# Moving the first quarter of the combined activations 64 bytes up in on-chip memory, onto the remainder of the weights that meet it

## The reference

```python
def conv_ffn(h, w_up, conv_w, conv_b, w_down):
    up = depthwise_conv(h @ w_up, conv_w, conv_b, FFN_CONV // 2)
    g, v = jnp.split(up, 2, axis=-1)
    return (jax.nn.gelu(g, approximate=True) * v) @ w_down

hx2 = modulate(rms_norm(x, g_ffn_pre[l]), sh2, sc2)
x = x + gt2 * rms_norm(conv_ffn(hx2, w_up[l], conv_ffn_w[l], conv_ffn_b[l], w_down[l]), g_ffn_post[l])
```

## Time and profile before

| what | value |
|---|---|
| median of three executions | 2101.1 us (2100.09 to 2101.67) |
| the profiled execution | 2102.9 us, span of its instructions 2101.1 us |
| TensorE matmul busy | 2066.7 us, 98% of the span |
| TensorE weight load busy | 1767.6 us, 84% |
| VectorE, ScalarE, GpSimd busy | 1529.7, 812.0, 79.0 us |
| granted TensorE clock, mean | 0.996 of full |

### The profile page before, as it was taken

One profiled execution on the slowest core, in us unless ns is written; L12 is line 12 of the kernel. 1 busy time (PEld: TensorE's weight loads), 2 busy tenths in 40 slices (PEclk: granted clock), 3 DMA queues, 4 the chain that ended last, 5 costly groups with the idle time before them and its releaser, 6 DMA issues.

```text
span 2101.1 us, 28297 instructions
## 1 busy us (share of the span) xinstructions
PE 2066.7 (98%) x11682; PEld 1767.6 (84%) x11682; DVE 1529.7 (73%) x2202; ACT 812.0 (39%) x1077; POOL 79.0 (4%) x145
## 2 busy tenths in 40 slices
PE   7999999999999999999999999999999999999998
PEld 4678887888777888888889898898988888888887
DVE  5567978876979886767767676676776768577577
ACT  5347576543323352423324243242333324233243
POOL 0000000001110000000000000000000000000002
PEclk9999999999999999999999999999999999999999
DMA  9953424434876524333333333434333333233342
GB/s 394 408 205 111 156 93 163 136 110 169 322 269 230 181 90 140 101 121 119 104 131 104 124 112 109 131 101 140 101 120 121 101 126 101 95 101 101 100 179 103
DMA packets 86193, 311.19 MB, mean 148 GB/s; under 512 B 9456, under 2 KB 13552, under 8 KB 84016
## 3 DMA queue, kind: packets, MB, share of 16 engines
q1 hardware_dynamic: 67824, 243.09, 33.3%
q0 software_dynamic: 17424, 65.50, 9.4%
q10 hardware_dynamic: 816, 0.79, 0.1%
HBM read 300.95 MB, written 8.39 MB: 147 GB/s over the span
## 4 chain that ended last, share of the span: by engine, by line
PE 68%; DVE 2%; DMA 1%; issue 1%; ACT 0%; DVEq 0%; ACTq 0%
PE bank L996 23%; PE bank L998 22%; PE bank L997 22%; DMA ada_raw<-in_adabg 1%; DVE w_lo L1540 1%; DVE acc L2175 0%; PE bank L1107 0%; DVE ada_acc L1572 0%; PE bank L1321 0%; DMA w_raw<-in_stream 0%; DVE x L1880 0%; DVE prod L1891 0%; ACT w_hi L610 0%; DVE ss L1548 0%; PE bank L1292 0%
## 5 line engine op out<-in xcount | busy, mean ns | idle before, releaser
L996 PE MATMUL bank<-h_hi,w_hi 128*128 128x512 f32 (+1 forms) x1968 | 711.1, 361 | 5.9 <-ACT acc L855 2.0
L997 PE MATMUL bank<-h_lo,w_hi 128*128 128x512 f32 (+1 forms) x1968 | 708.1, 360 | 0.0
L998 PE MATMUL bank<-h_hi,w_lo 128*128 128x512 f32 (+1 forms) x1968 | 706.5, 359 | 0.0
L1540 DVE TENSOR_TENSOR w_lo<-w_raw,w_hi 128x1024 fp32r<-128x1024 f32 x260 | 316.0, 1222 | 159.4 <-ACT w_hi L610 159.1
L996 PEld LDWEIGHTS bank<-h_hi,w_hi 128*128 128x128 f32 x1968 | 370.4, 188 | 65.5 <-issue 11.0
L610 ACT ACTIVATE w_hi<-w_raw 128x1024 fp32r<-128x1024 f32 x260 | 273.2, 1056 | 388.6 <-DMA w_raw<-in_stream 388.6
L998 PEld LDWEIGHTS bank<-h_hi,w_lo 128*128 128x128 f32 x1968 | 370.2, 188 | 56.8
L997 PEld LDWEIGHTS bank<-h_lo,w_hi 128*128 128x128 f32 x1968 | 372.8, 189 | 49.0
L996 PE MATMUL bank<-act_hi,w_hi 128*128 128x512 f32 (+1 forms) x688 | 265.0, 385 | 1.9 <-DVE acc L2147 1.5
L997 PE MATMUL bank<-act_lo,w_hi 128*128 128x512 f32 (+1 forms) x688 | 264.3, 384 | 0.0
L998 PE MATMUL bank<-act_hi,w_lo 128*128 128x512 f32 (+1 forms) x688 | 264.2, 384 | 0.0
(11 more groups left out here) (340 smaller groups left out, 2707.8 us busy)
## 6 DMA issues: line engine op xcount, KB each, us to landing
w_raw<-in_stream SPq DMA_DIRECT2D x340, 512.0 KB, 3.5
ada_raw<-in_adabg POOLq DMA_DIRECT2D x112, 512.0 KB, 4.7
ada_raw<-in_ada SPq DMA_DIRECT2D x64, 512.0 KB, 13.6
x<-in_x_t SPq DMA_DIRECT2D x4, 1024.0 KB, 8.4
acc<-in_adabg SPq DMA_DIRECT2D x8, 512.0 KB, 6.3
x<-in_x_t POOLq DMA_DIRECT2D x4, 1024.0 KB, 9.0
x_kept_d<-x SPq DMA_DIRECT2D x4, 1024.0 KB, 5.6
c<-in_ctx_t SPq DMA_DIRECT2D x2, 1024.0 KB, 14.1
```

The costliest lines, as they stand in the source:

```text
L996: t.matmul(out, w, v, start=start, stop=False)
L997: t.matmul(out, w, v_l, start=False, stop=False)
L998: return t.matmul(out, w_l, v, start=False, stop=stop)
L1540: v.tensor_tensor(lo_unit(n), raw_unit(n), hi_unit(n).bitcast(F32), ALU.subtract).then_inc(lo_done, 1)
```

## The change

The four quarters of `t` were one array of 4 x 768 elements, all at remainder 0. Now the array is 64 elements wider, the first quarter begins at element 16 (remainder 64 bytes) and the other three begin at 64 + 768 q (remainder 0, as before). The two arrays grow by 256 bytes each (`t_raw` and `t_lo` share one space). `up_sum` and `sums1_raw`/`sums1_lo` move up by 512 bytes, and the gap ahead of `acc` shrinks by that, so that `acc` and all behind it stay. No instruction, wait or transfer is added, removed or moved in order.

```diff
+T_AT = [16] + [64 + 3 * H * _q for _q in range(1, 4)]
+T_WIDTH = 4 * 3 * H + 64
...
-        t_raw, t_lo = twice(fin, "t_raw", "t_lo", [P, 4, 3 * H])
-        t_hi = sbuf(fin, "t_hi", [P, 4, 3 * H], F32R)
+        t_raw, t_lo = twice(fin, "t_raw", "t_lo", [P, T_WIDTH])
+        t_hi = sbuf(fin, "t_hi", [P, T_WIDTH], F32R)
         up_sum = sbuf(fin, "up_sum", [P, 2 * L])
         sbuf(fin, "gap_to_sums", [P, ASIDE])
         sums1_raw, sums1_lo = twice(fin, "sums1_raw", "sums1_lo", [P, NSUM])
-        sbuf(fin, "gap_to_x1", [P, 256 - ASIDE])
+        sbuf(fin, "gap_to_x1", [P, 256 - ASIDE - 128])
...
+        def three_of(t, q):
+
+            return t[:, ds(T_AT[q], 3 * H)]
+
+        def one_of(t, q, i):
+
+            return t[:, ds(T_AT[q] + i * H, H)]
...
-                a.activation(t_hi[:, q, :], t_raw[:, q, :], ACT.Copy).then_inc(t_rounded, 1)
+                a.activation(three_of(t_hi, q), three_of(t_raw, q), ACT.Copy).then_inc(t_rounded, 1)
...
-                    t4 = t_hi[:, q, 2 * H:3 * H], t_lo[:, q, 2 * H:3 * H]
+                    t4 = one_of(t_hi, q, 2), one_of(t_lo, q, 2)
...
-                    t2, t3 = ((t_hi[:, q, i * H:i * H + H], t_lo[:, q, i * H:i * H + H]) for i in range(2))
+                    t2, t3 = ((one_of(t_hi, q, i), one_of(t_lo, q, i)) for i in range(2))
...
-                t2, t3, t4 = (t_raw[:, q, i * H:i * H + H] for i in range(3))
+                t2, t3, t4 = (one_of(t_raw, q, i) for i in range(3))
...
-                v.tensor_tensor(t_lo[:, q, :], t_raw[:, q, :], t_hi[:, q, :].bitcast(F32), ALU.subtract).then_inc(t_ready, 1)
+                v.tensor_tensor(three_of(t_lo, q), three_of(t_raw, q), three_of(t_hi, q).bitcast(F32), ALU.subtract).then_inc(t_ready, 1)
```

## The result

The changed kernel takes 2089.85 us, the median of four executions (2089.1 to 2093.26), against 2101.16 us for the kernel before (2100.09 to 2101.67). The ratio is 0.9946, with a 95% interval of 0.9935 to 0.9958: 11.3 us or 0.5% faster. The forecast was no change that counts, 2101.9 us, and 2100.1 to 2103.8.

What follows compares the result with a forecast made beforehand. The prediction took TensorE's matmuls, busy throughout the feed-forward stage, as the bound. It summed +0.8 (matmuls) + 0 (making t) + 0 (moved sums) onto 2101.1 for 2101.9 us, range 2100.1 to 2103.8.

Steps and rivals of the forecast that it cites:

- What bounds the stage: Feed-forward stage, 750 to 2031 us: matmuls busy for all 1281.00 us, so every nanosecond of pitch goes into the time.
- The counts: Matmuls reading quarter 0: 9 in a pair, 360 in the kernel, one quarter of the 1440 that read `t`.
- The price at a lasting equal remainder: 256-column matmuls at equal remainders take 120.0 ns in the last down product, against 117.7 ns in the seven products.
- The moved sums: `up_sum` and the second set of sums move by 512 bytes and keep their remainders: zero cost.
- the instructions that make `t`: ScalarE's rounding (848 ns) and VectorE's subtracting (952 ns), near 730 us: costed at nothing, under 32 us of cover.
- The reason given for the sums: Matmuls against these sums and against ring slots show the same 281 ns and no idle time, so distance has no price.
- the 281 ns: Mean duration of the stage's matmul groups by shape, called no price because it overlaps with the next matmul.
- Price at steady pitch: Quarter 0's matmuls in the seven products: 360 x 2.3 ns = 0.8 us added, the prediction's own value.
- Rival 3: A small gain: short runs at equal remainders keep the early short pitch, 2100.7 us; chance 0.04.
- Rival 5: Faster by over 0.2%: 360 matmuls would need a pitch of 106 ns; chance 0.03, anything unforeseen included.
- the switching rival (4): Each of four switches of moving-operand remainder in a pair costs 0.033 us: 5.3 us, 2106.4 us; chance 0.05.

Runs made afterwards that it cites:

- e7: Kernel before, with the units of the seven products and their sums at remainder 0, so all 84 matmuls of a pair at equal remainders: 2109.13 us, ratio 1.0033.
- e1: Changed kernel, but all four quarters of t begin 256 bytes further up, with every remainder as in the kernel before: 2102.06 us, ratio 0.9994.
- e12: e6 with act_hi and act_lo 64 bytes lower, so down-product weights lie 64 bytes past what moves: 2099.32 us, ratio 0.9992 to the kernel before.
- e2: Changed kernel, but of the first quarter only t4 lies at remainder 64, t2 and t3 at 0: 2091.64 us, ratio 0.9944 to the kernel before.
- e3: Changed kernel, but of the first quarter only t2 and t3 lie at remainder 64, t4 at 0: 2093.51 us, ratio 0.9955 to the kernel before.
- e4: Changed kernel, but the third quarter lies at remainder 64 in place of the first: 2100.5 us, ratio 0.9989 to the kernel before.
- e6: e2 with the product on t4 of the first quarter put first of the 14 in its call: 2087.29 us, ratio 0.9927 to the kernel before.
- e9: e2 with t4 of the first quarter at remainder 32 in place of 64: ratio 0.9999 to the kernel before.
- e10: e2 with t4 of the first quarter at remainder 128 in place of 64: ratio 1.0001 to the kernel before.
- e5: Kernel before, with only the first matmul on t4 of the first quarter split into 192 and 64 columns: 2104.89 us, ratio 1.0015.
- e11: e6 with the first matmul on t4 of the third quarter also split into 192 and 64 columns: 2094.32 us, ratio 0.9965 to the kernel before.
- e8: Kernel before, with the units of the seven products and their sums 128 bytes up in place of 64: 2109.12 us, ratio 1.0036.

## Why the prediction was wrong

**Where it held.** What bounds the stage held: matmuls are busy without a gap from 750 to 2031 us after the change too, and every nanosecond of pitch is in the time. The counts held. The price at a lasting equal remainder held (e7: 119.9 ns). Of the nine matmuls of quarter 0 the three on t4 rose to 120 ns as forecast; the six on t2 and t3 did not. The moved sums cost nothing (e1), and the instructions that make `t` take 847 and 951 ns after the change, as before. The reason given for the sums was no proof, since it rested on the 281 ns that the prediction itself calls no price. Remainders alone move the pitch from 117.8 to 119.9 ns (e7) and at full width from 226.7 to 233.3 ns (e12). The Trainium skill, "TensorE: Matmul & The Clock Gate", section "Part 2: What happens when you issue a matmul", says that loading the next weights takes no read bandwidth from the running matmul; taken as the prediction took it, that a quarter may lie anywhere at no cost, these runs do not agree (2.1 and 6.6 ns a matmul). Whether it is the bandwidth that is short they do not show.

**The step that failed** is the one under "Price at steady pitch", 360 x 2.3 ns: it took 117.7 ns for the fixed price of the 3000 matmuls that the change leaves alone, and summed only over those that it touches. The 117.7 was one of two steady pitches. Matmuls whose operands have the remainders of before run at 113.3 ns once quarter 0 has gone by (places 17 to 26 and 36 to 83 of the trace after). Per pair: 0.01 us lost from t4 on, where eight matmuls take 0.95 us in place of 8 x 117.8 ns = 0.94; nothing from t2 on, where nine take 1234.56 - 1233.50 = 1.06 us as before; and 58 matmuls x 4.5 ns = 0.26 us gained in the two stretches at 113.3. That is 0.25 us a pair, 9.8 us over 40 pairs from the unrounded 0.245.

**What the prediction had in hand.** Rival 3 named a short pitch behind the full-width matmuls, but as something that the 360 might have. Rival 5 asked where 4.2 us could come from and looked only for 360 matmuls at 106 ns; 4.2 us is also 1.3 ns for all 3360 of the seven products. The rows held two hints that the slow rhythm was not the floor. The first: L997's weight loads at 192 ns among 188. The second: half of the full-width 226.7 ns is 113.3 ns, so 117.7 was 4 ns above what the same stream pays for half as many columns.

**Of the switching rival (4):** it had 0.033 us for each of four switches in a pair. The two around t4, with the five matmuls behind, cost 0.01 us together, those around t2 and t3 nothing over the slow pitch. The rhythm that follows decides.

**What is shown and what is not.** Shown: two steady pitches of matmuls with the same remainders; that t4 of quarter 0 at an equal remainder switches to the fast one (e2), t2 and t3 do (e3), and so does the third quarter (e4); the place of the switch sets the gain (e2, e4, e6), two other remainders of t4 do not switch (e9, e10), and a split does not (e5, e11). At waits of TensorE the pitch can switch too, either way (e12). Why an equal remainder does it, and why some waits do and others do not, is not shown. It can't be seen in the rows which access waits for which.

## What to carry to other kernels

Where TensorE is never idle, read the pitch of each shape from the timeline and compare it with half of the pitch at double width. If it lies above, the rhythm may be a slow one of two, as here, and a few matmuls may move thousands. This is one case, and a sign to look further, not a rule. Price an edit of operand places over all matmuls that follow until the rhythm is set anew, not over those it touches. Try the remainders of weights and moving operands as a pair, and for each width by itself, since the distance that is good for 256 columns cost 6.6 ns at 512.

## What the runs showed of the hardware

- Matmuls of 256 columns with weights 64 bytes past the moving operand (modulo 256) hold 117.8 or 113.3 ns, each for tens of matmuls, 106 at a time in one kernel (e12). At equal remainders and at 128 bytes all 84 of a pair average 120 ns (e7, e8). 256 bytes more under all of `t` change nothing (e1).
- Full-width matmuls hold 226.7 ns at equal remainders and 233.3 ns at 64 bytes (e12).
- After a split with a break of 0.2 us the pitch of before came back, slow in e5 and fast in e11. After waits of TensorE it came back in some places and changed in others (e12).
